# A gate matrix of experts built by accumulating single-word DMAs, with dense and gathering batches ranked together

## The reference, cut to what matters

```
q = (tb @ wq).reshape(PEER_BLOCK, PEER_HEADS, 2, PEER_QHALF)            # 8 heads
sc = jnp.einsum('thpd,hpnd->thpn', q, keys)                             # 2 x 128 scores a head
s1, i1 = lax.top_k(sc[:, :, 0], 16);  s2, i2 = lax.top_k(sc[:, :, 1], 16)
cand = s1[..., :, None] + s2[..., None, :]                              # 16 x 16 candidates
cidx = i1[..., :, None] * 128 + i2[..., None, :]
top_s, top_p = lax.top_k(cand, 16)                                      # 16 experts a head
eidx = take_along_axis(cidx, top_p);  g = softmax(top_s)
act = gelu(einsum('td,thkd->thk', tb, u_tab[eidx]))
out = einsum('thk,thkd->td', g * act, v_tab[eidx])
```

## Time and profile before

| | |
|---|---|
| median of 3 runs | 4115.0 us (4112.72 to 4124.71) |
| profiled execution | 4122.92 us, span 4121.1 us |
| PE busy | 3593.3 us, 87% |
| DVE busy | 2679.8 us, 65% |
| POOL busy | 1725.6 us, 42% |
| ACT busy | 1038.0 us, 25% |
| DMA | 1035.32 MB, mean 251 GB/s |

### The profile page before, as it was taken

The page is one execution under the profiler, slowest core; times in us unless marked ns, Lnnn a source line. Parts: engine busy times, 40 slices in busy tenths (PEclk is TensorE's granted clock), DMA queues, the critical chain, the costliest instruction groups (busy, mean ns, idle before and its releaser), DMA issues.

```text
span 4121.1 us, 43667 instructions
## 1 busy us (share of the span) xinstructions
PE 3593.3 (87%) x13392; PEld 1910.1 (46%) x13392; DVE 2679.8 (65%) x5438; ACT 1038.0 (25%) x2269; POOL 1725.6 (42%) x1506
## 2 busy tenths in 40 slices
PE   6998987788888777765999999999999999996656
PEld 4665743444444344453444444444444444442222
DVE  2443743234343578885887778777877777777875
ACT  1323531443344267741111111111111111110111
POOL 0000100000000067743666667666666666666541
PEclk9999999887778799987999999999999999998778
DMA  3000113776777423237999999999999999999862
GB/s 129 31 23 19 47 61 110 233 215 205 213 220 213 143 85 123 106 140 263 403 391 374 372 387 382 374 377 381 384 384 372 374 391 383 373 370 345 324 244 83
DMA packets 398895, 1035.32 MB, mean 251 GB/s; under 512 B 37821, under 2 KB 131230, under 8 KB 396642
## 3 DMA queue, kind: packets, MB, share of 16 engines
q0 software_dynamic: 165888, 604.05, 38.1%
q1 hardware_dynamic: 208658, 373.22, 27.2%
q10 hardware_dynamic: 24144, 55.58, 3.7%
HBM read 983.59 MB, written 49.09 MB: 251 GB/s over the span
## 4 chain that ended last, share of the span: by engine, by line
PE 45%; DMA 4%; DVE 3%; issue 1%; POOL 1%; SPq 0%; ACT 0%; DVEq 0%
PE e_b L1913 21%; PE e_b L1940 21%; PE e_b L1899 3%; DMA wq<-in_p_prompt 1%; DMA out_y_prompt<-w_room 1%; DMA wq<-in_peer_u 1%; PE e_b L2125 1%; DVE facc L2045 1%; DMA wq<-in_ple_gate_b 1%; POOL u L1999 0%; POOL v L2007 0%; DVE u L2017 0%; DMA u<-in_peer_u,idx_all 0%; DVE ln_st L939 0%; DVE w_room L950 0%
## 5 line engine op out<-in xcount | busy, mean ns | idle before, releaser
L1940 PE MATMUL e_b<-w_room,e_room 128*128 128x512 f32 x2048 | 901.5, 593 | 7.4 <-DVE k_room L1953 7.4
L1913 PE MATMUL e_b<-wq 128*128 128x512 f32 x2048 | 903.5, 594 | 0.0
L1999 POOL DMA_INDIRECT u<-in_peer_u,idx_all x576 | 734.1, 1275 | 391.4 <-DVE act L2017 170.8
L2007 POOL DMA_INDIRECT v<-in_peer_v,idx_all x576 | 678.7, 1178 | 439.5 <-DVE facc L2045 172.6
L2017 DVE CUSTOM_DVE_ANT_0 u<-u,xb 128x1024 f32<-128x1024 f32 x576 | 704.8, 1224 | 188.3 <-DMA u<-in_peer_u,idx_all 178.8
L1649 POOL TENSOR_SCALAR u<-iota,e_room 128x128 f32<-128x128 f32 x256 | 279.2, 1098 | 840.7 <-ACT e_room L1631 741.8
L1940 PEld LDWEIGHTS e_b<-w_room,e_room 128*128 128x128 f32 x2048 | 389.8, 190 | 499.1 <-issue 489.8
L1913 PEld LDWEIGHTS e_b<-wq 128*128 128x128 f32 x2048 | 380.8, 191 | 431.2 <-issue 431.2
L2045 DVE SCALAR_TENSOR_TENSOR facc<-v,w,facc 128x1024 f32<-128x1024 f32 x317 | 406.9, 1284 | 2.3
L1906 ACT ACTIVATE wq<-e_b 128x512 f32<-128x512 f32 x256 | 139.4, 594 | 835.5 <-PE e_b L1899 701.3
L2045 DVE SCALAR_TENSOR_TENSOR wq<-v,w,wq 128x1024 f32<-128x1024 f32 x254 | 326.0, 1283 | 0.5
(11 more groups left out here) (337 smaller groups left out, 4127.9 us busy)
## 6 DMA issues: line engine op xcount, KB each, us to landing
wq<-in_peer_u SPq DMA_DIRECT2D x128, 512.0 KB
w_room<-in_peer_v SPq DMA_DIRECT2D x128, 512.0 KB, 4.1
w_room<-in_cache_k SPq DMA_DIRECT2D x172, 256.0 KB, 3.0
w_room<-in_cache_v SPq DMA_DIRECT2D x172, 256.0 KB, 3.0
gate_scratch<-v ACTq DMA_DIRECT2D x16, 2048.0 KB, 6.3
wq<-gate_scratch SPq DMA_DIRECT2D x32, 1024.0 KB
u<-in_cache_k SPq DMA_DIRECT2D x84, 256.0 KB, 3.0
u<-in_cache_v SPq DMA_DIRECT2D x84, 256.0 KB, 3.0
```

The costliest lines, as they stand in the source:

```text
L1913: last = pe.matmul(AQ[c % 2][:, 0:DT], UT[c % 2][:, k, :], x1Td[:, k, :], start=(k == 0), stop=(k == KC - 1))
L1940: last = pe.matmul(OQ[i % 2][b][:], WT[n % 2][:, c, m * P:m * P + P], Vd[(4 * n + c) % NVD][:, b * 512:b * 512 + 512], start=(c == 0), sto ...
L1999: pool.indirect_dma_start(u[x % NU], None, a["peer_u"], bass.IndirectOffsetOnAxis(ap=idx_all[:, t, h, j:j + 1], axis=0)).then_inc(s_u[x % ...
L2007: pool.indirect_dma_start(v[y % NV], None, a["peer_v"], bass.IndirectOffsetOnAxis(ap=idx_all[:, t, h, j:j + 1], axis=0)).then_inc(s_v[y % ...
```

## The change

- The gate matrix is one array for each dense tile, [16,384 experts, 128 rows] (`gate_scratch0` to `3`, 8 MB each). SP stores zeros into all of it in 32 DMAs of 1 MB in prompt attention, behind the load of w_out; GpSimd first sets the zeros tile.
- After each dense batch VectorE also makes the word address of each choice, expert x 128 + row (`slot_of`). GpSimd adds each gate to its word with an indirect DMA of 128 single words: 16 choices x 4 tiles for each head. Within a head nothing is waited for; the first scatter into a tile waits until the head before has landed there.
- Split and one-hot steps, the stores and their waits go.
- There are still 16 batches for the prompt, in the order head 0 dense, head 0 gathering, head 1 dense, and so on; each head's wq is loaded once for both. Their query steps are spread over the sequences, 36 in each, and end in slot 241. Ranking steps are put into slots by a list of costs (`COST`, at 2.9 us a slot) that leaves out slots 16 and 17 of a sequence.
- The sample rows are one batch: heads 0 to 3 in partitions 0 to 63, heads 4 to 7 in 64 to 127. The eight small DMAs that moved them there go. Their chain stands in slots 257 to 289, and the list of slots ends at 290.
- x1's eight tiles have buffers of their own, are loaded between the first groups of pages, and turned in slots 0 to 7; the keys in 8 to 11.
- The gate loads have rows of 2 KB and are four DMAs.

```diff
-        gate_d = nc.dram_tensor("gate_scratch", (NDT * P // GB * PK, PK * GB), F32, kind="Internal").ap()
+        gate_d = [nc.dram_tensor(f"gate_scratch{n}", (PK * PK, P), F32, kind="Internal").ap() for n in range(NDT)]
...
 @block.sync   # prompt_attention
                 ahead(sp)
+                sp.wait_ge(s["zero"], 2)
+                for g in gate_d:
+                    flat = g.rearrange("(p e) t -> p (e t)", p=P)
+                    for n in range(0, PK * P, 2 * D):
+                        sp.dma_start(flat[:, n:n + 2 * D], zeros[:]).then_inc(s_gz, 16)
...
                 pool.memset(qz[:], 0.0).then_inc(s["zero"], 1)
-                pool.wait_ge(s["zero"], 1)
+                pool.memset(zeros[:], 0.0).then_inc(s["zero"], 1)
+                pool.wait_ge(s["zero"], 2)
...
+            if e < NBAT and group == 0:
                 ch.sync()
+                ch.add(dve.tensor_scalar(slot_of[:, :, h, :], idf[:], float(P), pcol[:], ALU.mult, ALU.add))
...
-        def split_pe(pe, n): ...
-        def quad_dve(dve, q): ...
-        def quad_pool(pool, q): ...
-        def quad_hot_act(act, q): ...
-        def quad_pe(pe, q): ...
-        def quad_act(act, q): ...
+        def scatter_pool(pool, h):
+            pool.wait_ge(s["tk"], 2 * h + 1)
+            if h == 0:
+                pool.wait_ge(s_gz, 16 * NDT * PK * P // (2 * D))
+            for j in range(TOPK):
+                for m in range(NDT):
+                    if j == 0:
+                        wait(pool, s_gs[m], 16 * TOPK * h)
+                    pool.indirect_dma_start(gate_d[m].rearrange("e (t o) -> (e t) o", o=1),
+                                            bass.IndirectOffsetOnAxis(ap=slot_of[:, m, h, j:j + 1], axis=0),
+                                            gd[:, m, h, j:j + 1], None, compute_op=ALU.add).then_inc(s_gs[m], 16)
...
-        Q_AT = {**{12 + n: (n,) for n in range(4)}, **{16 + n: range(4 + 3 * n, 7 + 3 * n) for n in range(4)}}
+        x, step = Q_FIRST, 0
+        while step < NBAT * 2 * KC:
+            c = x % SEQ_SLOTS
+            n = 3 if 16 <= c < 20 else 0 if c % 8 == 7 else 1
+            for _ in range(min(n, NBAT * 2 * KC - step)):
+                e, y = step // (2 * KC), step % (2 * KC)
+                Q_AT.setdefault(x, []).append((e, y))
...
+        COST = {"top": 1.6, "pairs": 2.0, "best": 1.5, "place": 1.7, "index": 3.7, "gate": 1.4}
...
         def load_g(sp, n):
             wait(sp, s["dW"], 4 * (n - 1))
-            src = gate_d.rearrange("(b p) (c t) -> p b c t", p=PK, t=GB)[:, :, 4 * n:4 * n + 4, :]
-            sp.dma_start(G[n % 2], src).then_inc(s_g[n % 2], 16)
+            for m in range(NDT):
+                if n == 0:
+                    sp.wait_ge(s_gs[m], 16 * PH * TOPK)
+                src = gate_d[m].rearrange("(p c) t -> p c t", c=PK)[:, 4 * n:4 * n + 4, :]
+                sp.dma_start(G[n % 2][:, m, :, :], src).then_inc(s_g[n % 2], 16)
...
 @block.gpsimd   # first block of peer
-                for q in range(NQUAD):
-                    quad_pool(pool, q)
+                for h in range(PH):
+                    scatter_pool(pool, h)
```

More of the change, by code:

```diff
@@ L1552, in peer @@
-        Q_AT = {**{12 + n: (n,) for n in range(4)}, **{16 + n: range(4 + 3 * n, 7 + 3 * n) for n in range(4)}}
-        def ranked_at(e):
-            if e < PH:
-                return SEQ_SLOTS * e + 26, 2 if e < PH - 1 else 1
-            return MIXED + RS * (e - PH) + 19, 1
-        def rank_steps(e):
-            at, pace = ranked_at(e)
-            steps = {at + pace * n: ("top", n) for n in range(2 * UN)}
-            at += 2 * UN * pace
-            for n, step in enumerate((("pairs", 0), ("best", 0), ("best", 1), ("best", 2), ("best", 3), ("place", 0))):
-                steps[at + n] = step
-            at += 6 if pace == 1 else 10
-            steps.update({at: ("index", 0), at + 1: ("index", 1), at + 3: ("gate", 0)})
-            return steps, at
@@ new lines, in peer @@
+        Q_OUT, SCORE_AT, SCORED_AT, RANK, EXP_AT = {}, {}, {}, {}, {}
+        for (e, m), x in Q_DONE.items():
+            Q_OUT[x + 1] = (e, m)
+        for e in range(NBAT + 1):
+            for r in range(2):
+                x = Q_DONE[e, 1] + 2 + 2 * r if e < NBAT else S_SCORE + r
+                SCORE_AT[x], SCORED_AT[x + 1] = (e, r), (e, r)
+        COST = {"top": 1.6, "pairs": 2.0, "best": 1.5, "place": 1.7, "index": 3.7, "gate": 1.4}
+        slot, used = 0, 0.0
+        for e in range(NBAT + 1):
+            ready = Q_DONE[e, 1] + 4 if e < NBAT else S_SCORE + 2
+            steps = [("top", n) for n in range(2 * UN)] + [("pairs", 0)] + [("best", n) for n in range(UN)] + [
+                ("place", 0), ("index", 0), ("index", 1), ("gate", 0)]
+            for name, n in steps:
+                first_slot = ready + (2 if name == "top" and n >= 4 else 0)
+                if slot < first_slot:
+                    slot, used = first_slot, 0.0
+                while used >= 2.5 or (slot < MIXED and slot % SEQ_SLOTS in (16, 17)):
+                    slot, used = slot + 1, max(0.0, used - 2.9)
+                RANK.setdefault(slot, []).append((e, name, n))
+                used += COST[name]
+                if (name, n) == ("index", 0):
+                    EXP_AT.setdefault(slot, []).append(e)
@@ L1829, in first_act @@
[L1829 to L1837 removed]
+            if X_TURN <= x < X_TURN + 2 * UN:
+                x_turn_act(act, x - X_TURN)
@@ L1838, in first_act @@
+            if x in SCORED_AT:
+                score_act(act, *SCORED_AT[x])
+            for e in EXP_AT.get(x, ()):
+                rank_gate_act(act, e)
+            step = {O_NORM: norm_act, O_MIX + 1: lambda act: ln.deviation(act, 0, SR), S_TURN: sample_turn_act}.get(x)
             if step:
@@ L2300, in _ @@
                 ch = Chain(dve, s["ch"])
-                for n in range(UN):
-                    x_turn_dve(dve, n)
-                dve.wait_ge(s["zero"], 1)
+                dve.wait_ge(s["zero"], 2)
                 ch.add(dve.tensor_tensor(ident2[:], ident[:, 0:SR], ident[:, SR:P], ALU.add))
```

426 lines of the change are left out of this document (153 added, 273 removed), and 3 rows, old and new, of the table names.

## The result

The changed kernel takes 4009.2 us (median of 4 runs, 4007.4 to 4012.3) against 4114.3 for the kernel before (4 runs, 4112.7 to 4124.7): ratio 0.974, 95% interval 0.9723 to 0.9757. It is faster by 105 us where 298 were forecast. The direction was right, and so was the engine that was named as the new bound; the size was not.

The account below looks back on a forecast made before the run. GpSimd's 512 scatters were taken as the new bound, ending at 1583 us: last stage 300 us earlier, +2 for the memset, so 4122.9 - 298 = 3825 profiled, 3817 us median. Range 3,735 to 4,090; the forecast's own 3,760 to 3,880.

Parts of the forecast that it names:

- The failed step: GpSimd's 512 scatters: 1.53 us each from start to start, 783 us in all, ending at 1583 us.
- Rival B: Accumulating form costs GpSimd 1.7 to 2.1 us a scatter, time about 4,000; chance 0.14.
- Rival C: Accumulating form costs GpSimd over 2.1 us a scatter; doubled building, 2.5 us, gives 4,303; chance 0.11.
- Rival A: Scatters cheap, 1.24 to 1.4 us each; the sample chain ends last, time 3,757; chance 0.25.
- Rival D: Words clog the DMA engines; at 151 ns a packet sequences become page-bound, time about 4,240; chance 0.10.
- The Trainium skill's fixed cost: Scatters: 2.0 us per DMA, one after the other, would take 1,024 us, for a time near 4,065.
- Sequences: Mixed stage, eight sequences: 87 to 88 us each where 84.2 before; bounds 80 and 106.
- The clock in value parts: Value parts of the sequences: clock mostly holds thanks to added query steps, over 0.8, saving 4 us a sequence.
- The sample chain: Sample rows' work behind the last sequence: 116 us, ending at 1523 us; bounds 1460 and 1680.
- Zero stores: 32 stores of 1 MB in prompt attention: landed by about 525 us, cost 0 us.
- The last stage: Dense and gathering stage at the end: unchanged but for its gate loads, 2,237 us long.
- Ranking of head 0: Mixed stage, slot 34: head 0 is ranked at about 800 us.

Follow-up runs that it names:

- 64 rows: Changed kernel with each scatter carrying 64 words of partitions 0 to 63 and not 128; 3944.4 us, ratio 0.9569.
- plain, spaced: Changed kernel with plain instead of accumulating scatters, a memset of 768 words and a wait for it behind each; 4099.7 us, ratio 0.9951.
- plain, spaced less: Changed kernel with plain instead of accumulating scatters, a memset of 192 words and a wait for it behind each; 3854.9 us (one run).
- two tiles: Changed kernel with scatters for only two of the four dense tiles, 256 of 512; 3798.4 us, ratio 0.9215.
- three tiles and products: Changed kernel with three dense tiles scattered (384) and the fourth tile's gates built by one-hot products; 3796.6 us, ratio 0.9213.

## Why the prediction was wrong, step by step

One view settles most of it: the first gather of the last stage, in each kernel, against its span.

| kernel | scatters, start to start | last scatter starts | first gather | span | span less first gather |
|---|---|---|---|---|---|
| changed | 512, 1.87 us | 1767.8 | 1775.6 | 4005.3 | 2229.7 |
| 64 rows | 512, 1.75 us | 1702.6 | 1708.5 | 3937.7 | 2229.2 |
| plain, spaced | 512, 2.05 us | 1855.8 | 1864.6 | 4095.4 | 2230.8 |
| plain, spaced less | 512, 1.57 us | 1612.2 | 1620.5 | 3852.8 | 2232.3 |
| two tiles | 256 | 1427.2 | 1563.8 | 3794.3 | 2230.5 |
| three tiles and products | 384, 1.89 us | 1536.2 | 1568.7 | 3804.7 | 2236.0 |

The last stage is the same to 3 us in the first five (the last row has a second multiply in each chunk and one more gate load); the time follows the scatters until the sample chain takes over at about 1564. With plain scatters back to back the stage is the same too (4389.0 - 2159.6 = 2229.4); there the slowed sequences decide, not GpSimd, whose last scatter starts at 1981.0.

- **The failed step: 1.53 us a scatter.** It is 1.87. That is 511 x 0.34 = 174 us of the 193 by which the gain fell short; the first scatter at 810 and not 800 adds 10. Most of the rest is that the profiled execution before stood 8.6 us above its median and the one after did not. The row behind the 1.53 was the mean of the plain gathers in the last stage, and it went wrong twice, in opposite directions. Of the 0.29 us that I put down to VectorE's work, 0.02 are there (mean 1.568, median 1.548), and 0.04 with plain scatters (1.004 and 0.963), though VectorE was busy 373 and 384 of 470 us. The longer records stand beside its products of 1.2 us (65 of 512, see the result); so it is these that count and not VectorE's busy share, and the ranking has few of them. Rival A had this argument, and it was right. And the accumulating form costs 0.59 us more, which I had left in the bounds alone. So the error of 0.34 is what is left of 0.59 too little, 0.27 too much and 0.02 by which a plain scatter is longer than a gather: it was luck that it was not larger. The bounds were 1.24 and 2.5; the truth lay at their middle, and I took a value near the low end because a row stood there. That row was of another form.
- **Rival B was what happened,** with its mechanism, its 1.7 to 2.1 us and its time of about 4,000. It had a chance of 0.14. With no row of the accumulating form, it deserved, in my judgement, at least the chance of the forecast.
- **Rival C,** building doubles, fell short: 0.59 us is 62% of the 0.95, and most of a record does not depend on the rows. The Trainium skill (GPSIMD Engine Reference, When to use GPSIMD) has one core write the read descriptors and another the write ones, which made doubling thinkable. It isn't contradicted by that, and no run shows the cores. Why the accumulating form costs more stays open.
- **Rival A** needed 1.4 us or less. Its place is right: with 256 scatters the sample chain ends last, at 1562.7, and the last stage starts at 1563.8.
- **Rival D** is out for the accumulating form: 37 to 48 ns a packet against my 40, DMA share 0.84, and 89.8 us a sequence. Its sign, digits of 9 in the DMA row of the mixed stage, did appear, so that sign was too weak: TensorE's waits for pages (weight loads and products added) grew only from 56 us in the stage to 85. Yet the danger behind it was real in a form I had not priced: plain transfers at 1.26 us stop the pages (4394.5 us), with the DMA share at 0.35. Had the change not needed the sum, the faster record would have made the kernel slower than before.
- **The Trainium skill's fixed cost** of some 2.0 us a DMA (DMA: Bandwidth & Descriptors, Anatomy of one DMA) taken as occupied time gave 4,065, nearer to 4,009 than my forecast. It was still the wrong reading: starts 1.26, 1.57, 1.75 and 1.87 us apart in four kernels show that no such cost runs one after the other.
- **Sequences:** forecast 87 to 88 us, 89.8 measured. The clock in value parts was forecast to hold mostly, and does (0.78 to 0.99) where there are query steps; without them it is 0.50.
- **The sample chain:** 116 us were forecast, and it took 1563.9 - 1424.4 = 139.5. Of the 23.5 too many, 24.5 are the sample queries (54.9 us for 30.4): TensorE had waited 13.4 us for w_out and 7.2 for the norm, and then was busy 55 of 56 us with the queries at clock 0.50. I had allowed 15 for that in the range and nothing in the sum. It cost nothing here, since GpSimd was later by 205 us.
- **Zero stores:** the stretch from 414 to 590 us has DMA 0.59 where the earlier trace rows has 0.08; the stores have landed by 510 us (525 forecast), and the mixed stage starts at 703.5 as forecast (703). Nothing, as costed. The memset record is 1.8 us for my 2.
- **The last stage:** 2,237 forecast, 1771 to 4005 measured: 2,234. **Ranking of head 0:** at 810 for 800.

## What to carry to other kernels

When a change adds hundreds of instructions of a form that the trace does not have, the price of one is the forecast. Don't take the nearest row for it if that row is of another form: give the dear case its share. Here the middle of the bounds, 1.87, happened to be right. A mean also carries its surroundings along: ask which instructions stood beside the slow records, and whether they stand beside yours. An indirect DMA's cost on GpSimd is in its count, so ask first how many are needed; when one engine's list sets the end of a stage in which the others fall idle, giving a quarter of it back to them by the old way can beat the version with all of it on that engine (3796.6 us against 4009.2; the kernel before, 4114.3, has none of it there but differs in more). And a run of narrow products at the lower clock is a good place for wider ones: here they cost next to nothing, as the clock rose with them.

## What the runs showed of the hardware that I had not expected

- An accumulating indirect DMA of 128 words occupies GpSimd for 1.55 us, a plain one for 0.96; an accumulating one of 64 words for 1.41. Between two stand 0.30 us in each form. Beside VectorE's products of two inputs and 1.2 us the 1.55 becomes 1.70 in the mean and up to 2.46.
- Plain indirect DMAs of 128 rows of 4 or 32 bytes, issued back to back (1.26 us from start to start), bring page loads and all compute engines nearly to a halt (TensorE busy 241 of 470 us where it was 428, sequences 166 us and not 90), with the DMA engines at 0.35. At 1.57 us from start to start, with a memset and a wait between, nothing of it is left (one run). The cause is open.
- A plain word DMA makes far fewer packets than an accumulating one: 182,272 in q0 over the whole kernel against 239,616, so (239616 - 182272) / 512 = 112 fewer for each.
- A row of 256 narrow products (64 columns) kept TensorE busy for 55 us, and the granted clock stayed at 0.50. With products of 128 columns put between them the same row began at 0.50 and rose: 0.87 over its stretch.
